# Two of the six weight chunks of an expert are loaded from ScalarE's DMA queue, the others from SyncE's

## What is computed

```python
def ec_moe(h, w_router, w_gate, w_up, w_down):
    cap = EC_CAPACITY * n // N_EXPERTS              # 2 * 512 // 16 = 64 tokens for an expert
    aff = jax.nn.softmax(logits, axis=1)
    g, idx = lax.top_k(aff, cap)
    xs = jax.vmap(lambda hb, ib: hb[ib])(h, idx)
    a = jnp.einsum('becd,edf->becf', xs, w_gate)    # 16 experts, each 1024 x 1024
    u = jnp.einsum('becd,edf->becf', xs, w_up)
    y = jnp.einsum('becf,efd->becd', jax.nn.silu(a) * u, w_down) * g[..., None].astype(h.dtype)
    # y is added to the rows idx of the output
```

## Time and profile before

| | |
|---|---|
| median of 3 runs | 1526.54 us (1525.84 to 1526.63) |
| profiled execution | 1529.07 us, of which the profile's span is 1527.3 us |
| TensorE busy | 1459.0 us, 96% of the span |
| VectorE, ScalarE, GpSimd busy | 48%, 15%, 5% |
| DMA | 504.52 MB, mean 330 GB/s |
| DMA in the stretches of the experts | 425 to 428 GB/s |

### The profile page before, as it was taken

The page is one execution under the profiler, slowest core; times in us unless marked ns, Lnnn a source line. Parts: engine busy times, 40 slices in busy tenths (PEclk is TensorE's granted clock), DMA queues, the critical chain, the costliest instruction groups (busy, mean ns, idle before and its releaser), DMA issues.

```text
span 1527.3 us, 16481 instructions
## 1 busy us (share of the span) xinstructions
PE 1459.0 (96%) x6796; PEld 678.4 (44%) x6796; DVE 734.6 (48%) x1299; ACT 234.4 (15%) x424; POOL 78.6 (5%) x70
## 2 busy tenths in 40 slices
PE   6999999999999999999889999999999999999997
PEld 4555656554433333333223688864333333333322
DVE  2578778766842322323222778777623232322222
ACT  2134453333300000000000300015100000000000
POOL 0010010000010000000000033000000000000000
PEclk9999999999999999999999999999999999999999
DMA  9953221668899999999999913177999999999996
GB/s 320 383 188 132 86 88 56 253 266 349 332 413 425 428 425 427 426 427 426 427 428 428 386 69 117 56 282 266 344 426 426 428 426 427 427 427 425 427 429 294
DMA packets 71172, 504.52 MB, mean 330 GB/s; under 512 B 8400, under 2 KB 18991, under 8 KB 42939
## 3 DMA queue, kind: packets, MB, share of 16 engines
q1 hardware_dynamic: 66778, 489.84, 79.0%
q0 software_dynamic: 2592, 8.39, 1.5%
q10 hardware_dynamic: 1728, 5.24, 0.9%
HBM read 497.16 MB, written 6.29 MB: 330 GB/s over the span
## 4 chain that ended last, share of the span: by engine, by line
PE 72%; DMA 21%; DVE 5%; issue 1%; ACT 1%; SPq 1%; DVEq 0%; POOLq 0%; ACTq 0%
PE ps L1294 29%; DMA ring<-in_exp_w_up_dram 13%; PE ps L1388 9%; PE ps L1097 6%; DMA work<-in_exp_w_up_dram 6%; PE ps L1304 6%; PE ps L994 3%; PE ps L953 2%; PE ps L785 2%; PE ps L898 2%; PE ps L894 2%; PE ps L957 1%; PE ps L980 1%; DMA ring<-in_ada_w_dram 1%; PE ps L1261 1%; PE ps L1340 1%
## 5 line engine op out<-in xcount | busy, mean ns | idle before, releaser
L1294 PE MATMUL ps<-ring,small 128*64 128x512 f32 x1680 | 376.0, 595 | 17.4 <-DMA ring<-in_exp_w_gate_dram 11.7
L1294 PE MATMUL ps<-work,small 128*64 128x512 f32 x1360 | 304.9, 595 | 13.3 <-DMA work<-in_exp_w_gate_dram 9.7
L2422 DVE TENSOR_TENSOR work<-ps,work 128x1024 f32<-128x1024 f32 x120 | 141.4, 1220 | 308.5 <-PE ps L1304 308.5
L1294 PEld LDWEIGHTS ps<-ring,small 128*64 128x64 f32 x1680 | 116.9, 137 | 264.9 <-issue 228.8
L1294 PEld LDWEIGHTS ps<-work,small 128*64 128x64 f32 x1360 | 94.5, 137 | 216.7 <-issue 184.8
L1304 PE MATMUL ps<-small 64*128 64x512 f32 x480 | 127.4, 628 | 0.0
L2431 DVE TENSOR_TENSOR small<-small,ps 128x512 f32<-128x512 f32 x32 | 22.0, 688 | 151.2 <-issue 150.1
L1691 ACT ACTIVATE small<-ps 128x512 f32<-128x512 f32 x32 | 19.1, 597 | 471.4 <-PE ps L1294 471.4
L2440 DVE SCALAR_TENSOR_TENSOR small<-ps,gate_e,gate_ffn 128x512 f32<-128x512 f32 x32 | 24.0, 751 | 128.1 <-PE ps L1294 128.1
L2617 POOL DMA_INDIRECT small<-xn_rows,row_no x30 | 28.8, 961 | 987.2 <-PE ps L1261 674.7
L1695 ACT ACTIVATE small<-ps 128x512 f32<-128x512 f32 x32 | 19.1, 597 | 345.2 <-PE ps L1340 345.2
(11 more groups left out here) (381 smaller groups left out, 1521.3 us busy)
## 6 DMA issues: line engine op xcount, KB each, us to landing
ring<-in_exp_w_down_dram SPq DMA_DIRECT2D x35, 2048.0 KB, 29.9
ring<-in_exp_w_gate_dram SPq DMA_DIRECT2D x32, 2048.0 KB, 32.5
ring<-in_exp_w_up_dram SPq DMA_DIRECT2D x30, 2048.0 KB, 35.8
work<-in_exp_w_up_dram SPq DMA_DIRECT2D x28, 2048.0 KB, 31.8
work<-in_exp_w_gate_dram SPq DMA_DIRECT2D x28, 2048.0 KB, 28.7
work<-in_exp_w_down_dram SPq DMA_DIRECT2D x27, 2048.0 KB, 35.1
ring<-in_ada_w_dram SPq DMA_DIRECT2D x34, 1024.0 KB, 8.5
ring<-in_exp_w_up_dram SPq DMA_DIRECT2D x6, 1024.0 KB, 8.7
```

Of the source, the lines that this page charges most:

```text
L1294: last = mm(PS[64 * h:64 * h + 64, bank, :], lhsT[:, m * P + 64 * j:m * P + 64 * j + 64], aside[m][h] if n == ASIDE else slot_rows[sl][:, ...
L2422: v.tensor_tensor(row, PS[:, b:b + 2, :], row, ALU.add).then_inc(added[L], 1)
```

## The change

`BY_ACT` lists the chunks whose slot was freed by a chunk 6e+1 or 6e+3 with e of 1 or more. `load_ring` of SyncE leaves them out. ScalarE issues them itself, in `load_after`: the one after its SiLU of expert e, the other after its copy of the turned rows of expert e, behind a wait on `used[L]` that the copy's own wait has met already. Since the ring has 11 slots, these are chunks 6k and 6k+2 for k from 3 to 15 (the first half of a gate matrix, the first half of an up matrix): 26 in a layer, 52 in all. Nothing else changes.

```diff
+        BY_ACT = [n for n in RING[SLOTS:] if place_before(n) >= 6 and place_before(n) % 6 in (1, 3)]
@@
             def load_ring(L):
                 for n in RING[SLOTS:]:
+                    if n in BY_ACT:
+                        continue
                     if L == 0 and place_before(n) == ASIDE + 1:
                         sp.wait_ge(used[0], ASIDE + 1)
                         load_mix_bias(1)
@@
+            def load_after(L, before):
+                for n in BY_ACT:
+                    if place_before(n) == before:
+                        act.dma_start(slot_rows[slot_of(L, n)], chunk_rows(L, n)).then_inc(slot_in[slot_of(L, n)], 16)
+
             def experts(L):
@@
                     f(hid, PS[:, 0, :], ACT.Silu).then_inc(silu_ok, 1)
+                    load_after(L, 6 * e + 1)
                     act.wait_ge(hid_T[L], e + 1)
                     if e >= 1:
                         act.wait_ge(used[L], 6 * e)
                     f(hidT, PS[:, 3, :], ACT.Copy).then_inc(hidT_ok[L], 1)
+                    act.wait_ge(used[L], 6 * e + 4)
+                    load_after(L, 6 * e + 3)
```

## The result

The changed kernel takes 1552.39 us (median of 5 runs, 1551.37 to 1556.5) against 1526.54 us before (median of 5, 1522.52 to 1527.14): 25.9 us more, a ratio of 1.0175 with a 95% interval of 1.016 to 1.0189. The forecast was 1547.9 us, in a range of 1535 to 1558, and slower.

What follows compares the result with a forecast made beforehand. DMA engines that never pause bound the experts until chunk 93 lands, then 13.46 us of TensorE's work; the change only reorders landings. 10.7 us in each of two layers, 21.4, on 1526.5 gave 1547.9 us, range 1535 to 1558.

Steps and rivals of the forecast that it cites:

- The issues on ScalarE cost nothing: In the experts, 52 issues of 0.33 us fit ScalarE's idle gaps of about 11 and 15 us: zero.
- A late start costs nothing, with at most 3.8 us a layer: Loads start 0.7 and 3.1 us later, but the queue is never empty: zero, at worst 3.8 us a layer.
- The 0.5% lost in going between two queues: Upper bound in the experts: DMA engines lose 0.5% over some 400 us a layer, 4 us, giving 1552.
- A chunk on ScalarE's queue passes SyncE's: In the experts, two queues get half each, so ScalarE's chunk lands some 12 us after issue, against 48.8 on SyncE's.
- the 10 to 14 that were to show it: Sign in the experts: ScalarE's chunks land in 10 to 14 us, SyncE's still in over 40.
- The price is set by the last wait and TensorE's work from there: At each layer's end, the last wait is at chunk 85 with 48.7 us of work behind: 10.7 us more a layer.
- The waits fell on second halves: Sign in the experts: waits begin around the ninth expert, on second halves (6e+1, 6e+5), never on ScalarE's chunks.
- Layer 0's loss isn't hidden: Layer 0 ends like layer 1 and the convolution's first product moves with TensorE's end: its 10.7 us counts in full.
- nothing takes the 10.7 us back: After layer 0, the convolution's weights land when they did and its first product comes later, so 10.7 us stays.
- the convolution, put at 0: The forecast's sum held only the two layers' 10.7 us each, with no term for the convolution.
- Two queues moved no more bytes: Rival in the experts: a second queue carries more bytes and removes TensorE's waits, at most to 1499.5 us; 6 in 100.
- ScalarE's queue got its half, where a third was needed: Rival in the experts: ScalarE's queue gets clearly under a third or long holds, some 38 us a layer, near 1600; 5 in 100.

Runs made afterwards that it cites:

- e10: The changed kernel with, in layer 1 only, all chunks from 60 to 95 issued in order on ScalarE's queue: 1536.92 us, ratio 1.0066.
- e3: The changed kernel with ScalarE's queue kept only for chunks below 60 (experts 3 to 9), 14 of 26 a layer: 1526.46 us, ratio 0.9999.
- e4: The changed kernel with only chunks 84, 86, 90 and 92 of each layer on ScalarE's queue: 1557.05 us, ratio 1.0199.
- e8: e4 with each of its four chunks a layer issued one expert later: 1534.87 us, ratio 1.0059.
- e6: The changed kernel with ScalarE's transfers in layer 0 only, layer 1 loading as before: 1541.06 us, ratio 1.0104.
- e5: The changed kernel with GpSimd's scaling of the convolution's output weights held until VectorE's third triple of weight sums is made: 1548.95 us, ratio 1.0154.
- e2: The changed kernel with only the transfer after the copy (chunks 6k+2) on ScalarE's queue: 1547.98 us, ratio 1.0151.
- e12: e2 with GpSimd's scaling held until the third triple's weight sums are made, as in e5: 1540.35 us, ratio 1.0091.

## Why the prediction was right, step by step

*The issues on ScalarE cost nothing.* Right. They take 0.33 us, SiLU and copy keep their 0.60 us, and with 36 issues in one layer ScalarE was never held for more than 0.69 us at one (e10).

*A late start costs nothing, with at most 3.8 us a layer.* Right. The experts' slices carry what they did. The first window of layer 1 has 413 GB/s where it had 429, with a DMA share of 1.00: an estimate from these is 0.9 us, and 93 landed 0.5 us late against its layer's start. The 0.5% lost in going between two queues, a bound of the forecast, came from no row and no run shows it: the slices keep their 426 to 427 GB/s.

*A chunk on ScalarE's queue passes SyncE's.* Right. The share was half, as I took it (53.8 and 47.7% from 1468 to 1476). Landing took 14.5 us at the median where 12 was my figure, mostly outside the 10 to 14 that were to show it: the part ahead of the first bytes was taken too small, over 3 us for chunk 90, and the gather takes a share too, 11.7% from 1480 to 1484 while 92 is moved. It is still far below 40.

*The price is set by the last wait and TensorE's work from there.* Right in place and size: chunk 85, 48.70 us, and 10.0 and 11.3 us instead of 10.7. The waits fell on second halves of gate and down alone and began in layer 1 with the chunks 47 and 49, as foretold. There is luck in the place: the step needed chunk 92 to be in before 85, and with the longer landing it was so by 0.1 us in layer 1 (1491.5 and 1491.6) and by 0.4 in layer 0 (807.5 and 807.9). With a slightly later landing of 92 the bytes between 85 and 93 would have been others, and the sum with them. e3 and e4 show that it is this and nothing that adds up over the transfers: 28 early ones cost 0.6 us, 8 late ones 31.2. e8 shows that it is the time of landing and not the queue or the issue: the same eight cost 8.7 when issued later.

*Layer 0's loss isn't hidden.* Right (e6). But "nothing takes the 10.7 us back" was not the whole: the weights that kept their time became a cause. This is the term that was too small: the convolution, put at 0, measured 4.0 us in the profile (4.9 at the product that waits), and e5 shows the cause. The forecast looked for what the unmoved weights would hide, and not for who starts work as soon as they land.

*The size.* 21.4 forecast, 25.9 measured. The convolution makes 4 of the difference. The layers' two terms sum to 21.3 us in the profiles. The profiled execution of before was 2.5 us over its median, and 2.0 of these lay ahead of layer 0 (412.08 against 410.08). So the stages from layer 0 on account for 25.3 of the 25.9 us.

*The rivals.* Two queues moved no more bytes, and ScalarE's queue got its half, where a third was needed. The Trainium skill (*DMA: Bandwidth & Descriptors*, *Issuing engines are not separate DMA queues*) says that transfers of several engines interleave on the same DMA engines and that issuing them so only saves the sequencer's time. The slices agree with the first. The second doesn't hold here: with some ten chunks in line on the one queue the order of landing changes, and that cost 25.9 us.

## What to carry to other kernels

Where the DMA engines are the bound, a second queue was no second road here but a priority: what is issued on the short queue passes what waits in the long one. Don't put there what is needed last, above all not in the last stretch, where there is no time left to use what came early. Whether it helps to put there what is needed first, no run here tried. To price such a change, find the last transfer that the busy engine waits for and add up its work from there; and look which other engine starts on a landing that now comes early against the rest.

## What the runs showed of the hardware that was not expected

- A VectorE addition of 128x512 with both inputs in SBUF took 0.69 us alone and 1.6 to 1.75 us while GpSimd's 128x512 product in SBUF ran (L2490 to L2493 beside L2651). The Trainium skill, *SBUF — State Buffer*, *SBUF: two separate sides*, has it that a VectorE operation with two inputs in SBUF and a GpSimd operation that reads SBUF lock each other out of a shared pair of ports, for a whole instruction. The rows fit it, though they don't show the lock: GpSimd's eight operations take 12.29 / 8 = 1.54 us each, and a VectorE addition next to them about as long as one of those, while the VectorE operations with an input in PSUM keep their 0.41 us (L2527 at 881.96).
- A wait of TensorE of some us within the experts was often followed by a stretch at 1.2 GHz: 16 records in 5.1 to 6.4 us instead of 3.65 (at 1431.42 in the changed kernel after 2.41 us of waiting, with a mean granted clock of 0.69 from 1431 to 1436.5; at 1478.09 in e2, at 808.16 in e12), 1.4 to 2.7 us each. Not after every such wait: of the seven of 2.2 us or more in the changed kernel's experts three were, and 3.07 us at 1483.72 left the clock as it was. Before the last wait of a layer it may cost nothing, behind it it counts in full.
- A 2 MB transfer on ScalarE's queue moved no bytes for over 3 us after its issue (issued at 1464.71, none up to 1468).
- With three queues at work the gather landed in 10.8 us at the median instead of 8.4.
